# First expert's row numbers by a product of one column, and the second table moved behind four units

## What is computed

```python
logits = x2 @ w_router + b_router              # 32 experts
top_val, top_idx = lax.top_k(logits, 4)        # each token goes to 4 of them
gates = softmax(top_val)
# for each expert e, on the rows of the tokens that chose it:
gu = xb @ w_gu[e] + b_gu[e]                    # 1024 -> 2048
hmid = min(gate, 7) * sigmoid(1.702 * gate) * (clip(up, -7, 7) + 1)
y = hmid @ w_down[e] + b_down[e]               # 1024 -> 1024
# y times the gate is added up over a token's 4 experts; y = LN2(alpha * h + sum)
```

## Time and profile before

| | us |
|---|---|
| median of 3 runs | 1273.67 (1271.19 to 1275.38) |
| the profiled execution | 1274.26 |
| its span | 1272.3 |
| TensorE busy | 1202.4 (95%) |
| VectorE busy | 1050.8 (83%) |
| ScalarE busy | 945.9 (74%) |
| GpSimd busy | 174.6 (14%) |
| moved by DMA | 475 MB, mean 373 GB/s |

### The profile page before, as it was taken

One profiled execution on the slowest core, in us unless ns is written; L12 is line 12 of the kernel. 1 busy time (PEld: TensorE's weight loads), 2 busy tenths in 40 slices (PEclk: granted clock), 3 DMA queues, 4 the chain that ended last, 5 costly groups with the idle time before them and its releaser, 6 DMA issues.

```text
span 1272.3 us, 35060 instructions
## 1 busy us (share of the span) xinstructions
PE 1202.4 (95%) x15390; PEld 870.7 (68%) x15390; DVE 1050.8 (83%) x1202; ACT 945.9 (74%) x1260; POOL 174.6 (14%) x145
## 2 busy tenths in 40 slices
PE   7999998899999999999999999999999999999985
PEld 3555555677777777777777777777777777777742
DVE  6565566899988889998988888888888888888886
ACT  5433311688989888988888888888888888888821
POOL 1264210111101000100100001111111111101002
PEclk9999998899999999999999999999999999999997
DMA  9662394599999999999999999999999999999983
GB/s 364 230 246 85 108 419 164 219 363 414 426 425 424 426 425 423 425 426 426 425 426 425 424 425 425 426 425 424 424 426 424 426 424 427 424 423 427 401 351 95
DMA packets 46839, 475.00 MB, mean 373 GB/s; under 512 B 8701, under 2 KB 9620, under 8 KB 20828
## 3 DMA queue, kind: packets, MB, share of 16 engines
q1 hardware_dynamic: 34636, 438.58, 82.3%
q0 software_dynamic: 11392, 31.77, 6.6%
q10 hardware_dynamic: 656, 2.36, 0.5%
HBM read 452.99 MB, written 29.95 MB: 380 GB/s over the span
## 4 chain that ended last, share of the span: by engine, by line
PE 40%; DMA 27%; DVE 9%; issue 4%; ACT 4%; DVEq 0%; SPq 0%; ACTq 0%
PE wide L1010 28%; DMA ring<-in_w_gu 16%; PE bank L1010 11%; DMA ring<-in_w_down 8%; DVE work L1840 5%; ACT work L874 3%; DMA work<-part_rows 2%; PE bank L1319 1%; ACT work L904 1%; DVE ring L1975 1%; DVE ring L1973 1%; DVE work L1770 0%; DVE ring L1962 0%; DVE work L1831 0%; DVE work L1825 0%
## 5 line engine op out<-in xcount | busy, mean ns | idle before, releaser
L1840 DVE SCALAR_TENSOR_TENSOR work<-ring,work 128x2048 f16<-128x2048 f32 x320 | 721.3, 2287 | 108.6 <-ACT work L874 97.0
L874 ACT ACTIVATE work<-ring 128x2048 f16<-128x2048 f32 x320 | 599.6, 1902 | 86.1 <-DMA ring<-in_w_gu 60.0
L1010 PE MATMUL wide<-work 128*128 128x96 f16 (+2 forms) x7024 | 482.2, 229 | 33.9 <-DVE work L1825 8.6
L1010 PEld LDWEIGHTS wide<-work 128*128 128x128 f16 (+2 forms) x7024 | 372.2, 101 | 128.5 <-issue 44.0
L1010 PEld LDWEIGHTS bank<-work 128*128 128x128 f16 (+4 forms) x6530 | 299.2, 100 | 40.6 <-issue 26.3
L1010 PE MATMUL wide<-ring,work 128*96 128x512 f32 (+3 forms) x1004 | 326.4, 491 | 0.0
L1010 PE MATMUL bank<-work 128*128 128x96 f16 (+4 forms) x6530 | 310.0, 208 | 10.0 <-DVE work L1770 3.0
L1010 PEld LDWEIGHTS wide<-ring,work 128*96 128x96 f32 (+3 forms) x1004 | 128.6, 134 | 172.1 <-issue 122.0
L687 POOL DMA_INDIRECT work<-h_rows,work x32 | 61.3, 1916 | 463.7 <-PE bank L1319 446.5
L700 POOL DMA_INDIRECT part_rows<-work x30 | 42.7, 1422 | 371.8 <-ACT work L934 371.8
L904 ACT ACTIVATE work<-bank,work 128x96 f32<-128x96 f32 x256 | 65.1, 334 | 0.0
(11 more groups left out here) (207 smaller groups left out, 591.5 us busy)
## 6 DMA issues: line engine op xcount, KB each, us to landing
ring<-in_w_gu SPq DMA_DIRECT2D x128, 2048.0 KB, 29.2
ring<-in_w_down SPq DMA_DIRECT2D x64, 2048.0 KB, 31.9
part_rows<-work POOLq DMA_DIRECT2D x1, 10240.0 KB, 37.2
ring<-part_rows SPq DMA_DIRECT2D x3, 2560.0 KB, 26.7
ring<-in_w_in SPq DMA_DIRECT2D x3, 2048.0 KB, 13.2
ring<-in_w_out SPq DMA_DIRECT2D x2, 2048.0 KB, 10.6
h_rows<-work POOLq DMA_DIRECT2D x1, 2560.0 KB, 9.9
ring<-h_rows SPq DMA_DIRECT2D x1, 2560.0 KB, 23.4
```

Of the source, the lines that this page charges most:

```text
L874: act.activation(whi[buf(n, p)], packed(s, p), ACT.Copy, scale=W_UP).then_inc(hi_done, 1)
L1010: return pe.matmul(out, w, x, start=start, stop=stop, skip_group_check=True)
L1840: dve.scalar_tensor_tensor(wlo[buf(n, p)], packed(s, p), W_UP, whi[buf(n, p)], ALU.mult, ALU.subtract).then_inc(split_done, 1)
```

## The change

- **GpSimd**: `xg` is set to zero before the wait for the stored rows; the waits for the states and for `zeroed` and both `iota` come behind the issue of the first gather.
- **VectorE**: the two copies into `used` come before `route` of the last tile. Behind it come the comparisons of expert 0 for tiles 0 to 3, `rank_tile(4)`, the comparison for tile 4, and only then `gate_info(4)`, in the middle of which `first_ids` takes the token numbers from a new product. `rows_of(0)` no longer makes them. Comparisons for table 1 come between the splits of pairs 2 and 3, `rows_of(1)` and `places_of(0)` behind pair 3. The counts are copied with table 2.
- **TensorE**: a product of the comparisons with the token number's column alone (five products of one column) with a semaphore of its own; `idle` of 9, 4, 3, 4 and 4 products where there were 14, 4, 8 and 12; table 1 and the product that selects the places of expert 0 behind unit 3 of expert 0, table 1 without the counts, which go to table 2.
- **SP**: `b_gu` comes first, and (0,4) and (0,5) go behind the first gather's landing, where (1,2) follows.

```diff
--- before.py
+++ after.py
@@ -340,7 +340,7 @@
         passed = sem("passed")
         ov_setup, ov_known, ov_pick = sem("ov_setup"), sem("ov_known"), sem("ov_pick")
         ov_place = sem("ov_place")
-        acc_out, ln2_in = sem("acc_out"), sem("ln2_in")
+        ids_ready, ln2_in = sem("ids_ready"), sem("ln2_in")
         y_done, y_stored = sem("y_done"), sem("y_stored")
 
         N_SMALL, N_LATER = 6, 5
@@ -527,13 +527,14 @@
             sp.wait_ge(wo_lo, 8)
             for e, i in ((0, 0), (0, 1), (0, 2), (0, 3), (1, 0), (1, 1)):
                 load(e, i, piece_slot(e, i))
-            sp.wait_ge(mix_ready, TILES)
-            for i in (4, 5):
-                load(0, i, piece_slot(0, i))
             sp.wait_ge(hT_ready, 2 * TILES)
             sp.wait_ge(h_stored, 16 * TILES)
             sp.dma_start(bguT[:, 0:E, :], b_gu).then_inc(late_in, 16)
+
+            sp.wait_ge(mix_ready, TILES)
             sp.wait_ge(gathered[0], 16)
+            for i in (4, 5):
+                load(0, i, piece_slot(0, i))
             for e in range(1, E):
                 for i in range(2 if e == 1 else 0, PER):
 
@@ -667,15 +668,9 @@
                 pool.wait_ge(var_ready, t + 1)
                 pool.tensor_tensor(small[0:n, 48 + t:49 + t], small[0:n, 48 + t:49 + t],
                                    small[0:n, 64:65], ALU.pow).then_inc(std_ready, 1)
-            pool.wait_ge(states_out, 96)
-            pool.wait_ge(h_stored, 16 * TILES)
             pool.wait_ge(mix_ready, TILES)
             step(pool.memset(xg, 0.0))
-            pool.wait_ge(zeroed, 32)
-            pool.iota(val_e, pattern=[[1, E], [0, MAXB - 1]], base=0, channel_multiplier=0,
-                      allow_small_or_imprecise_dtypes=True).then_inc(made, 1)
-            pool.iota(val_b, pattern=[[0, E], [BLK, MAXB - 1]], base=BLK, channel_multiplier=0,
-                      allow_small_or_imprecise_dtypes=True).then_inc(made, 1)
+            pool.wait_ge(h_stored, 16 * TILES)
 
             def gather(m, q, q2):
 
@@ -702,6 +697,12 @@
                                         oob_is_err=False).then_inc(scattered, 16)
 
             gather(0, 0, 0)
+            pool.wait_ge(states_out, 96)
+            pool.wait_ge(zeroed, 32)
+            pool.iota(val_e, pattern=[[1, E], [0, MAXB - 1]], base=0, channel_multiplier=0,
+                      allow_small_or_imprecise_dtypes=True).then_inc(made, 1)
+            pool.iota(val_b, pattern=[[0, E], [BLK, MAXB - 1]], base=BLK, channel_multiplier=0,
+                      allow_small_or_imprecise_dtypes=True).then_inc(made, 1)
             gather(1, 1, 1)
             for n in range(E):
                 if n + 2 < E:
@@ -1279,21 +1280,31 @@
                 mix(t, 1, range(3, 4))
             pe.wait_ge(mix_used, TILES - 1)
             positions(TILES - 2)
-            idle(14)
+            idle(9)
             h_columns(TILES - 1)
             logits(TILES - 1)
             idle(4)
             positions(TILES - 1)
-            idle(8)
+            idle(3)
+
+
+            pe.wait_ge(hot_ready, 1)
+            for t in range(TILES):
+                n = ROWS[t]
+                last = mm(bank[0][:, 488:489], hot[0:n, t, :], info[0:n, t, 0, 3:4], t == 0, t == TILES - 1)
+            last.then_inc(ids_ready, 1)
+            idle(4)
 
             def table(m, e):
 
-                pe.wait_ge(hot_ready, m + 1)
+                pe.wait_ge(hot_ready, m + 2)
                 if not isinstance(m, int) or m > 0:
                     pe.wait_ge(table_copied, m)
-                if not isinstance(m, int) or m > 1:
+                if isinstance(m, int) and m == 1:
+                    pe.wait_ge(gT_out, 2)
+                elif not isinstance(m, int) or m > 1:
                     pe.wait_ge(gT_out, m * 2 - 2)
-                if isinstance(m, int) and m == 1:
+                if isinstance(m, int) and m == 2:
                     for t in range(TILES):
                         n = ROWS[t]
                         mm(bank[0][:, 448:448 + E], ones[0:n, :], member[0:n, t, :], t == 0, t == TILES - 1)
@@ -1303,15 +1314,16 @@
                               t == 0, t == TILES - 1)
                 last.then_inc(table_ready, 1)
 
+            def select(m):
+                mm(bank[0][0:BLK, 484:488], used16, found[m % ROW_BUFS if isinstance(m, int) else 0], True, True)\
+                    .then_inc(sel_ready, 1)
+
             def rows(m, q, got, tables):
 
                 pe.wait_ge(table_copied, tables)
                 if not isinstance(m, int) or m > 0:
                     pe.wait_ge(dst_known, m)
-                else:
-                    pe.wait_ge(bias_ready, 1)
-                mm(bank[0][0:BLK, 484:488], used16, found[m % ROW_BUFS if isinstance(m, int) else 0], True, True)\
-                    .then_inc(sel_ready, 1)
+                    select(m)
                 pe.wait_ge(gathered[q], got)
                 for b in range(2):
                     for k in range(4):
@@ -1373,12 +1385,15 @@
                 last.then_inc(down_read, 1)
 
             table(0, 0)
-            table(1, 1)
-            idle(12)
-            rows(0, 0, 16, 2)
+            idle(4)
+            rows(0, 0, 16, 1)
             for n in range(E):
                 for u in range(8):
                     unit(n, u, n % 2)
+                    if n == 0 and u == 3:
+                        pe.wait_ge(bias_ready, 1)
+                        select(0)
+                        table(1, 1)
                 if n + 2 < E:
                     table(n + 2, n + 2)
                 if n + 1 == E:
@@ -1661,6 +1676,18 @@
                 dve.tensor_reduce(mem, each.rearrange("p k e -> p e k"), AX.X, ALU.add).then_inc(routed, 1)
                 dve.wait_ge(routed, t + 1)
 
+            def first_hot(tiles):
+
+                for t in tiles:
+                    n = ROWS[t]
+                    last = dve.tensor_scalar(hot[0:n, t, :], iota16[0:n, :], rank[0:n, t, 0:1], None, ALU.is_equal)
+                return last
+
+            def first_ids():
+
+                dve.wait_ge(ids_ready, 1)
+                dve.tensor_scalar(tok_i[0], bank[0][:, 488:489], float(PLACES), None, ALU.add).then_inc(rows_known, 1)
+
             def gate_info(t):
                 n = ROWS[t]
                 g4 = small[0:n, 16:20]
@@ -1670,6 +1697,8 @@
                 step(dve.reciprocal(small[0:n, 21:22], small[0:n, 20:21]))
                 step(dve.tensor_scalar(g4, g4, small[0:n, 21:22], 1.0 / ALPHA, ALU.mult, ALU.mult))
                 step(dve.tensor_tensor(each_g, each, g4.unsqueeze(2).to_broadcast([n, TOPK, E]), ALU.mult))
+                if t + 1 == TILES:
+                    first_ids()
                 step(dve.tensor_reduce(gate, each_g.rearrange("p k e -> p e k"), AX.X, ALU.add))
                 step(dve.tensor_scalar(info[0:n, t, 0:E, 0], gate, W_UP, None, ALU.mult))
                 step(dve.scalar_tensor_tensor(info[0:n, t, 0:E, 1], gate, W_UP, info[0:n, t, 0:E, 0],
@@ -1742,9 +1771,16 @@
             dve.sem_inc(hm_done, 2)
             dve.sem_inc(out_ready, 1)
             dve.sem_inc(unit_used, BUFS)
+
+            four = ident.rearrange("p (g d) -> p g d", d=4)
+            step(dve.tensor_copy(used[:, 0:BLK].rearrange("p (g d) -> p g d", d=3), four[:, :, 0:3]))
+            step(dve.tensor_copy(used[:, BLK:P].rearrange("p (g d) -> p g d", d=1), four[:, :, 3:4]))
             route(TILES - 1)
+            first_hot(range(TILES - 1))
+            rank_tile(TILES - 1)
+            first_hot([TILES - 1]).then_inc(hot_ready, 1)
             gate_info(TILES - 1)
-            rank_tile(TILES - 1)
+            dve.nop().then_inc(hot_ready, 1)
 
             def counts():
 
@@ -1775,12 +1811,13 @@
                 dve.wait_ge(table_ready, m + 1)
                 if last is not None:
                     dve.wait_ge(scattered, last * 16 + 16)
-                if isinstance(m, int) and m == 1:
+                if isinstance(m, int) and m == 2:
                     step(dve.tensor_copy(count, bank[0][:, 448:448 + E]))
                 dve.tensor_copy(found[q], bank[0][:, 480:484]).then_inc(table_copied, 1)
                 dve.wait_ge(table_copied, m + 1)
-                dve.tensor_scalar(tok_i[q], found[q][:, 3:4], float(PLACES), None, ALU.add)\
-                   .then_inc(rows_known, 1)
+                if not isinstance(m, int) or m > 0:
+                    dve.tensor_scalar(tok_i[q], found[q][:, 3:4], float(PLACES), None, ALU.add)\
+                       .then_inc(rows_known, 1)
 
             def places_of(m, q):
 
@@ -1843,19 +1880,12 @@
             def next_lo(n, p):
                 lo(n, p, piece_slot(n, p // 2))
 
-            onehot(0, 0)
+            rows_of(0, 0, None)
             step(dve.memset(iota16_back, -1.0))
             by_four = [x.rearrange("p (g d) -> p g d", d=4)[:, :, 0:3] for x in (iota16, iota16_back)]
             step(dve.tensor_scalar(by_four[1], by_four[0], -1.0, BLK + 1.0, ALU.mult, ALU.add))
```

(13 more changed lines are left out.)

## The result

| | kernel before | changed kernel |
|---|---|---|
| median (us) | 1272.43 (1271.00 to 1275.38, 4 runs) | 1283.85 (1282.36 to 1284.59, 4 runs) |
| ratio | | 1.0073, 95% interval [1.0056, 1.0091] |
| span of the profiled execution | 1272.3 | 1280.5 |

The change makes the kernel slower by 0.73%, about 9 us, where 1.2 us less was forecast. The forecast's range ended at 1277.0. The two medians above lie further apart, 11.4 us, but they are of four runs each: in the runs of the experiments the kernel before had medians of 1274.46, 1274.61 and 1274.77 us over 27 to 29 runs.

The account below looks back on a forecast made before the run. At 300 to 1180 us the weight stream bounds the kernel, with two gates at its head. The second gate decides: 1.2 us less, profiled execution 1274.26 to 1273.1, median 1273.67 to 1272.5 us; range 1269.0 to 1277.0.

Parts of the forecast that it names:

- the second gate: Expert 0's down, which (2,1)'s issue waits for at the stream's head: 1.2 us earlier, setting the end.
- what GpSimd's zeros could cost VectorE: Zeros of xg moved beside the last tile's norm: 0 us taken, 0.45 us as the other end.
- Rival B: Cold clock and slow second gather, landing at 257.7: down 1.5 us later, 1275.2 us; chance 0.15.
- The two gates: Stream's restart and the end of expert 0's down, before 300 us; a shift of both passes through to the end.
- The first gate: Stream's restart at its head, moved to the first gather's landing at 230.4: 3.8 us less lost time.
- VectorE's wait for table 1: Ahead of rows_of(1), behind unit 3: table at 241.85 against VectorE at 239.8, cutting pair 4's 3.3 us gain to 1.2.
- the 5 us at half rate: TensorE's assumed time at 1.2 GHz around expert 0's first units, putting table 1 at 241.85.

Follow-up runs that it names:

- the kernel with one wait more: Kernel before, with GpSimd's second gather made to wait for VectorE's fourth split: 1284.50 us, ratio 1.0078.
- an earlier gather: Changed kernel with table 1 (without counts), its comparisons and rows_of(1) ahead of the first split: 1273.33 us, ratio 0.9987; with places product and places_of(0) too: 1273.76 us, 0.9997.
- VectorE's short wait: Changed kernel; VectorE waits behind places_of(0), ahead of table 2's comparisons, until GpSimd has issued the second gather: 1274.09 us, ratio 1.0003.

## Why the prediction was wrong

**The step that failed** is one sentence of the second gate: "The second gather begins at 243.5 instead of some 238, and lands 12.0 later at 255.5". It began at 242.46 and landed 21.8 us later, at 264.28. The 12.0 was the median of 32 gathers of the kernel before, 3.7 to 12.9, and I took their highest value as the bound. Of the 21.8 us, 11.14 are the issue, for 1.0 to 2.8 in those 32. But none of those 32 was issued where comparisons give way to a run of splits. In the kernel before the second gather was issued beside the rows' low halves, which read PSUM; the change moved `rows_of(1)` to just ahead of table 2's comparisons and four splits, with two gated products among them and no gap. A range over like instructions bounds the cost of a moved one only if it meets the same neighbours.

**The neighbours were asked about, in one direction only.** The text priced what GpSimd's zeros could cost VectorE (0 to 0.45 us) and found that a split isn't slowed. It never asked what the split does to GpSimd. The rule that it cited, the Trainium skill's "GPSIMD Engine Reference" (Specifications), names contention with instructions that have two inputs in SBUF, and the split is one: for the gather's issue the runs agree with it, by 11.14 for 1.04 us. The splits took their usual time while GpSimd waited.

**Rival B had the place and not the price.** It put the loss at the second gather, with 12.9 us as the end, and gave 1.5 us. The landing was 21.8. With that number its own working comes near the result: 242.46 + 21.8 = 264.3 for the transposes, TensorE at a low clock behind them, `down` 10 us late.

**Two small slips in the sums** decide nothing. By the steps around it the second gather would begin at 241.85 + 0.4 + 0.9 = 243.15 and not 243.5, and table 0 with its copy ends at 227.6 and not 227.75 (measured: 228.0).

**What held.**
- The two gates. Down's distance grew by 10.2 us, and the ratio makes 9.3 us of the time; in the kernel with one wait more it grew by 10.3 and the ratio was 1.0078. The stream behind 300 us passed it on.
- The first gate: token numbers 226.06 (225.8), gather 227.03 (226.7), (0,4) at 230.76 (230.4), first units 235.23 (234.6).
- The second gate but for the gather: VectorE's wait for table 1 was 0.95 us, with PEclk 0.50 between 236 and 238 and 1.00 from 240. The rise came sooner than the 5 us at half rate that I took (the three rows above make it about 3.4 us), and the start was 0.6 us later than forecast. Without the gather's delay `down` came 1.36 us earlier, for 1.2; that these are so near is in part luck, since the two misses pull in opposite directions.
- That SP's part is worth nothing: in three pairs of kernels, undoing it changed the ratio by +0.16%, +0.11% and -0.06%.
- The time that a lead of 1 to 3 us at the second gate gives is not resolved. With 1.36 the ratio was 1.0003, with 1.2 it was 0.9997, with 2.0 and 2.6 it was 0.9991 twice, each within 0.10% to 0.14%; and with `down` 0.8 us later it was 0.9987. That every microsecond there comes out at the end is shown for the loss of 10 us and only argued for a gain of 1.

**What stays open.** That the gather's long issue makes the loss is shown: the loss goes with it in three ways (a later run of splits, a gap, an earlier gather) and comes with it in the kernel before. Why the issue is held is not. It got through with the first split 0.65 us behind its start (in all three kernels with VectorE's short wait) and not with 0.40 or less, so some step of it in that stretch is met by the split, but which one, and why it then passes by the starts of five further instructions that free a gather begun amid a split, no run tells. The short wait itself (0.17 us, over at 242.28, ahead of the issue's row at 242.45) was not tried apart from the 0.25 us by which it shifts the split. Nor was a shorter run of splits, nor one behind something else than comparisons. Most other gathers begin amid a split and last 1.0 to 2.8 us; the one at 258.17 in the kernel before ended at 260.61, 0.94 behind the start of the gated product (259.67). The gap of 0.03 us behind that product (at 260.22) came too late to be what let it go on, since it took some 0.9 us from the gap that was put in.

## What to carry to other kernels

Before a step is moved on VectorE, look at what GpSimd is released to do by it, and at what VectorE runs from there for the next microseconds. Here a gather whose issue was met, within 0.4 us of its start, by the change from comparisons to a run of float32 operations with two SBUF inputs waited out the whole run. What helped in these runs: the run held back by 0.25 us, to 0.65 us behind the gather's start; the gather issued amid earlier splits; or one gap (a wait for VectorE's own result) behind the first split. And where a bound is taken from like instructions, ask whether any of them had the neighbours that the moved one will have.

## What the runs showed that was not expected

- The issue of an indirect DMA on GpSimd, 1.0 us by itself, lasted 11.14, 11.14 and 10.64 us in three kernels when VectorE's splits followed its comparisons 0.4 us behind the issue's start or with it, and ended 0.94 to 1.00 us behind the first small copy. With the splits 0.65 us behind its start it lasted 1.04, in three kernels.
- Begun amid a split, it ended 0.85 to 1.00 us behind the start of VectorE's next instruction (359 of 361 gathers), also where that was another split with no gap before it (1.29 us in all in one kernel).
- With a gap of a few hundredths of a microsecond put between the first two splits of the run it ended some 0.9 us behind the gap (3.60 us in all, for 11.14).
- VectorE shows nothing of it: its splits take 2.28 us beside the waiting instruction as they do elsewhere. Only GpSimd's row and the landing tell.
